# Expert rows through DRAM by indirect DMA, expert weights in loads of 512 columns, and every lower part on VectorE

## The reference

```
probs = softmax(h @ router); top_p, top_i = top_k(probs, 2); top_p /= sum(top_p)
combine = sum(one_hot(top_i) * top_p)                      # weight of a token for an expert
hid = silu(h @ w_gate[e]) * (h @ w_up[e]) * combine[..., e]   # w_gate, w_up: 8 x 1024 x 1408
f = sum over e of hid @ w_down[e]                          # w_down: 8 x 1408 x 1024
x = x + gate2 * rmsnorm(f, norms[3])
```

## Time and profile before

| | us |
|---|---|
| median of 3 timed runs | 2277.51 (2275.06 to 2282.47) |
| the profiled execution | 2269.22 |
| its span, first to last instruction | 2267.3 |
| TensorE busy | 2089.9 (92%) |
| VectorE busy | 1180.6 (52%) |
| ScalarE busy | 893.9 (39%) |
| GpSimd busy | 387.4 (17%) |
| expert loop, first product to last copy | 1619.66 to 2232.42 |
| moved by DMA | 354.66 MB |

### The profile page before, as it was taken

The page is one execution under the profiler, slowest core; times in us unless marked ns, Lnnn a source line. Parts: engine busy times, 40 slices in busy tenths (PEclk is TensorE's granted clock), DMA queues, the critical chain, the costliest instruction groups (busy, mean ns, idle before and its releaser), DMA issues.

```text
span 2267.3 us, 36209 instructions
## 1 busy us (share of the span) xinstructions
PE 2089.9 (92%) x15258; PEld 1771.2 (78%) x15258; DVE 1180.6 (52%) x1505; ACT 893.9 (39%) x1210; POOL 387.4 (17%) x274
## 2 busy tenths in 40 slices
PE   4899899999979999869989999997799999999996
PEld 2898788885549999859878888655588888888875
DVE  1955345543064342387534554214666666676774
ACT  2345522231142222233462223202466666566653
POOL 2600123220000000063003333000022222221112
PEclk7899899999979999989989999997799999999998
DMA  9322012236443434652111212645199888889981
GB/s 326 138 75 79 1 39 95 76 109 217 148 149 120 140 100 127 200 193 89 66 38 39 64 69 93 232 175 163 45 283 296 279 276 276 277 275 289 284 273 45
DMA packets 305234, 354.66 MB, mean 156 GB/s; under 512 B 4937, under 2 KB 245601, under 8 KB 304608
## 3 DMA queue, kind: packets, MB, share of 16 engines
q1 hardware_dynamic: 303456, 346.56, 46.9%
q0 software_dynamic: 1664, 6.41, 0.9%
HBM read 346.66 MB, written 6.29 MB: 156 GB/s over the span
## 4 chain that ended last, share of the span: by engine, by line
PE 79%; DVE 10%; ACT 4%; DMA 4%; issue 3%; DVEq 0%; POOL 0%; SPq 0%; ACTq 0%; POOLq 0%
PE bank L1341 6%; PE bank L1342 6%; PE bank L1343 6%; PE bank L1224 5%; PE bank L871 5%; PE bank L1096 4%; PE bank L873 4%; PE bank L872 4%; PE bank L1237 4%; PE bank L1253 4%; PE bank L1251 4%; PE bank L1252 4%; PE bank L1318 3%; PE bank L907 3%; PE bank L908 3%
## 5 line engine op out<-in xcount | busy, mean ns | idle before, releaser
L873 PE MATMUL bank<-hT_hi,ring_split 128*128 128x384 f32 x576 | 195.3, 339 | 0.0
L1402 ACT ACTIVATE ring_split<-ring 128x1024 fp32r<-128x1024 f32 (+2 forms) x86 | 119.7, 1411 | 166.9 <-DMA ring<-in_ffn_w_up 109.8
L559 POOL TENSOR_TENSOR ring_split<-ring,w_upper_a 128x1536 fp32r<-128x1536 f32 (+1 forms) x20 | 63.5, 3197 | 593.6 <-ACT w_upper_a L554 593.6
L554 ACT ACTIVATE w_upper_b<-ring 128x2048 fp32r<-128x2048 f32 (+2 forms) x80 | 124.0, 1563 | 96.5 <-PE bank L1343 96.5
L559 DVE TENSOR_TENSOR ring_split<-ring,w_upper_a 128x2048 fp32r<-128x2048 f32 (+2 forms) x60 | 135.0, 2291 | 46.4 <-ACT w_upper_a L554 46.4
L554 ACT ACTIVATE w_upper_a<-ring 128x2048 fp32r<-128x2048 f32 (+1 forms) x80 | 129.4, 1642 | 71.0 <-PE bank L1343 71.0
L2096 DVE TENSOR_TENSOR ring_split<-ring,ring_split 128x2048 fp32r<-128x2048 f32 (+1 forms) x30 | 74.1, 2503 | 145.7 <-ACT ring_split L1402 145.7
L1342 PE MATMUL bank<-ring_split,xg_hi 128*128 128x512 f32 (+1 forms) x400 | 148.6, 371 | 0.0
L871 PE MATMUL bank<-hT_hi,ring_split 128*128 128x384 f32 x384 | 141.2, 368 | 4.3 <-DVE modv L1801 2.9
L909 PE MATMUL bank<-ring_split,hT_hi 128*128 128x256 f32 x480 | 138.6, 289 | 0.0
L1402 ACT ACTIVATE work<-bank 128x256 f32<-128x256 f32 (+2 forms) x131 | 52.9, 448 | 214.9 <-PE bank L1096 86.5
(11 more groups left out here) (356 smaller groups left out, 5503.7 us busy)
## 6 DMA issues: line engine op xcount, KB each, us to landing
ring<-in_w_in SPq DMA_DIRECT2D x28, 2048.0 KB, 9.0
ring<-in_ada_w SPq DMA_DIRECT2D x24, 2048.0 KB, 10.2
ring<-in_moe_w_down SPq DMA_DIRECT2D x30, 1408.0 KB, 6.1
ring<-in_moe_w_gate SPq DMA_DIRECT2D x40, 1024.0 KB, 7.2
ring<-in_moe_w_up SPq DMA_DIRECT2D x40, 1024.0 KB, 9.7
oT<-in_moe_w_down SPq DMA_DIRECT2D x10, 1408.0 KB, 6.2
ring<-in_w_branch SPq DMA_DIRECT2D x8, 1536.0 KB, 17.5
ring<-in_ffn_w_gate SPq DMA_DIRECT2D x11, 1024.0 KB, 5.5
```

Of the source, the lines that this page charges most:

```text
L554: nc.scalar.activation(m_half(w_upper[j % 2], j, h), m_half(m_place(j), j, h), ACT.Copy).then_inc(mw_hi, 1)
L559: op.tensor_tensor(m_half(m_place(j, True), j, h), m_half(m_place(j), j, h), m_half(w_upper[j % 2], j, h).bitcast(F32), ALU.subtract).then ...
L873: last = mm(out, lo, hT_hi[:, k], start=False, stop=k == KT - 1)
```

## The change

The rows of an item and its result now pass through two DRAM tensors, `xslots` and `yslots`, of 14 x 128 rows of 1024. Both are filled with zeros once, by SP from the cleared DeltaNet state, ahead of the load of w_in block 9: xslots in layer 0, yslots in layer 1. GpSimd writes every token's row to its two slots with six indirect DMAs, SP reads the 128 rows of the next item into `xs`, and TensorE transposes them (`turn_rows`). Only item 0 is still gathered by products. SP stores each item's result to `yslots` (`store_out`). At the end GpSimd reads the two result rows of every token back with six indirect DMAs, and ScalarE and VectorE weigh and add them, and make norm, gate and residual in the row layout; the residual stays in the banks, transposed by TensorE. Selection, weighted selection, scatter and the adds of every item are gone.

Loads 0 to 5 now come in pairs: 512 columns of gate and up (the last pair 384) by 4 row tiles; loads 6 to 9 hold 512 columns of down by 6 or 5 row tiles. Gate and up go to a bank each. SiLU, gate product and the transposes of hidden are made once for each pair. VectorE makes all lower parts. What SP, GpSimd and the two row layouts do at the end is in the diff:

```diff
-            return (2, KT, 256 if j < M_GU - 1 else P) if j < M_GU else (1, FE, 256)
+            return (2, 4, 512 if j < M_GU - 2 else 384) if j < M_GU else (1, 6 - j % 2, 512)
...
+                if kind == "w" and at[1] == 9:
+                    sp.wait_ge(s_zero, at[0] + 1)
+                    sp.dma_start((xslots, yslots)[at[0]].rearrange("(i p) n -> p i n", p=P),
+                                 RX[:, 6144:7168].unsqueeze(1).to_broadcast([P, NI, D])).then_inc(zero_out, 16)
...
+                if j == M_SLOT + 1:
+                    for done in moved:
+                        sp.wait_ge(done, 32)
+                    sp.dma_start(xs, xslots[P:2 * P, :]).then_inc(xs_in, 16)
...
                     moe_load(e, j)
+                    if j == M_SLOT:
+                        store_out(i - 1)
+                        sp.wait_ge(ga_mm, 2 * i + 2)
+                        sp.dma_start(xs, slot_rows(xslots, i + 1)).then_inc(xs_in, 16)
+            store_out(last_item)
...
-            with pool.Fori(0, n_items) as i:
-                for j in POOL_U:
-                    for h in range(M_HALF):
-                        m_lower(pool, nc.gpsimd, j, h, i, mp_lo)
+            pool.wait_ge(route_ok, 5)
+            for t in range(NT):
+                for j in range(TOP_K):
+                    pool.indirect_dma_start(xslots, row_at(t, j), h2tok[:, t], None).then_inc(moved[t], 16)
...
+            pool.wait_ge(ys_out, 32 * n_items + 1)
+            link(nc.gpsimd.tensor_tensor(place2, place2, place2, ALU.subtract))
+            for t in range(NT):
+                for j in range(TOP_K):
+                    pool.indirect_dma_start(yrow[j][:, t], None, yslots, row_at(t, j)).then_inc(moved[t], 16)
...
-                            if j == 0:
-                                scatter(i)
-                            else:
-                                turn_hidden(j - 1, i)
...
-                        gather(0)
-                        turn_hidden(M_GU - 1, i)
-                        gather(1)
+                            if j in (2, 4):
+                                turn_hidden(b - 1, i)
+
+                        pe.wait_ge(xs_in, 16 * i + 16)
+                        for half in range(2):
+                            turn_rows(half)
+                        turn_hidden(M_BLK - 1, i)
...
+            def scaled(t):
+                act.wait_ge(moved[t], 64)
+                go(yrow[0][:, t], yrow[0][:, t], ACT.Copy, scale=m8[:, 8 * t:8 * t + 1]).then_inc(y_a, 1)
...
+                    v.tensor_tensor(esel, slot1.unsqueeze(1).to_broadcast([P, NT, SLOTS]), bc(rank[:, :, 0], SLOTS),
+                                    ALU.is_equal).then_inc(route_ok, 1)
...
+                        for b in range(M_BLK - 1):
+                            lower(2 * b + 2, i)
+                            if b:
+                                hidden_lower(b - 1, i)
+                            half_lower(2 * b + 3, 0, i)
+                            hidden_gate(b, i)
+                            half_lower(2 * b + 3, 1, i)
...
+            def y_add(t):
+                wait(dve, "root", DEPTH - 1, 4 + t)
+                link(v.reciprocal(vss[:, t:t + 1], vss[:, t:t + 1]))
+                link(v.scalar_tensor_tensor(yrow[0][:, t], yrow[0][:, t], vss[:, t:t + 1], grow[:, 0 if t == 0 else 1], ALU.mult, ALU.mult))
+                dve.wait_ge(xo_mm, 4 + t + 1)
+                v.tensor_tensor(yrow[0][:, t], yrow[0][:, t], banks[:, 512 * X_BANK[t]:512 * X_BANK[t] + D], ALU.add).then_inc(xo_ev, 1)
```

More of the change, by code:

```diff
@@ L1320, in gather, with turn_rows @@
                         last.then_inc(ga_mm, 1)
[L1322 to L1329 removed]
+                    def turn_rows(half):
+                        for m in range(4 * half, 4 * half + 4):
+                            last = tr(B[4 + half][:, (m % 4) * P:(m % 4 + 1) * P], xs[:, m * P:(m + 1) * P])
+                        last.then_inc(ga_mm, 1)
@@ L1382, in _ @@
                             for h in range(M_HALF):
                                 m_split(pe, j, h, i)
-                                product(out, j, h, ehid_hi, ehid_lo).then_inc(dn_mm, 1)
-                    scatter(n_items)
-                    sum_squares(layer, 4, sqP)
+                                product([B[OUT_BANK[(j - M_GU) // 2]][:, :]], j, h, ehid_hi, ehid_lo, FE).then_inc(dn_mm, 1)
                 ada_units(at["n4"], 6, ada_buf)
-            wait(pe, "xk", DEPTH, 0)
-            for t in range(NT):
-                for half in range(2):
-                    for k in range(4):
-                        last = tr(B[2 + 2 * t + half][:, k * P:(k + 1) * P], xT[:, 4 * half + k, t * P:(t + 1) * P])
-                    last.then_inc(xo_mm, 1)
+            pe.wait_ge(mod_ok, 4 * DEPTH)
@@ new lines, in _ @@
+            for q, b in enumerate((0, 1, 6, 7)):
+                g, half = divmod(q, 2)
+                for k in range(4):
+                    last = mm(B[b][:, k * P:(k + 1) * P], mod[:, DEPTH - 1, 5, 4 * half + k, g:g + 1].to_broadcast([P, P]), ident,
+                              start=True, stop=True)
+                last.then_inc(xo_mm, 1)
+            for t in range(NT):
+                if t:
+                    pe.wait_ge(y_a, 2 * t)
+                else:
+                    pe.wait_ge(ga_lo, 2 * n_items + 2)
+                for k in range(KT):
+                    last = tr(banks[:, 512 * X_BANK[t] + k * P:512 * X_BANK[t] + (k + 1) * P], xT[:, k, t * P:(t + 1) * P])
+                last.then_inc(xo_mm, 1)
@@ new lines, in item_upper @@
+                        gate_silu(M_BLK - 1, i)
+                        ahead(M_GU - 1, 0, i)
+                        hidden_upper(M_BLK - 1, i)
+                        ahead(M_GU - 1, 1, i)
+                        gathered(i + 1)
+                        for j in range(M_GU, M_GU + 2):
+                            for h in range(M_HALF):
+                                ahead(j, h, i)
+                        act.wait_ge(ys_out, 32 * i + 1)
+                        out_half(0, i)
+                        if not last:
+                            for h in range(M_HALF):
+                                ahead(M_GU + 2, h, i)
@@ L1749, in _ @@
+                        out_half(1, i)
+                        if not last:
+                            for h in range(M_HALF):
+                                ahead(M_GU + 3, h, i)
                     for j in range(2):
@@ L1757, in _ @@
                     item_upper(last_item, True)
-                    act.wait_ge(sc_ad, KT * n_items + KT + 1)
-                    for k in range(KT):
-                        square(yT, sqP, k)
+                    break
                 root(layer, 4)
@@ new lines, in place_rows @@
+                    def place_rows():
+                        link(v.tensor_scalar(nit, e_lo, float(SLOTS), -1.0, ALU.mult, ALU.add))
+                        link(v.tensor_tensor(ranked, rank, nit.unsqueeze(1).to_broadcast([P, NT, NE]), ALU.add))
+                        for pk in picks:
+                            last = v.tensor_tensor(pk, pk, ranked, ALU.mult)
+                        link(last)
+                        for j, pk in enumerate(picks):
+                            last = v.tensor_reduce(place2[:, :, j], pk, AX.X, ALU.add)
+                        link(last)
+                        v.tensor_copy(row_of, place2.rearrange("p t j -> p (t j)")).then_inc(route_ok, 1)
```

314 lines of the change are left out of this document (158 added, 156 removed).

## The result

| | before | after |
|---|---|---|
| median of the timed runs, us | 2276.99 (2275.06 to 2282.47, 4 runs) | 2141.18 (2139.86 to 2144.84, 4 runs) |
| ratio, 95% interval | | 0.9402 (0.9382 to 0.9423) |
| span of the profiled execution | 2267.3 | 2138.4 |
| expert loop, first product to end of the last copy | 613.4 | 495.2 |
| one turn of it | 61.42 | 49.53 |

The changed kernel is 6.0% faster, 135.8 us by the medians. The prediction was 2145 within 2128 to 2188.

A forecast was written before the change was run, and what follows sets the result against it. TensorE was taken to bound the expert loop, transfers next. From 2269.2 us, minus 114 (loop), 7.3 (ahead of it) and 11.2 (end), came 2136.7; with 8.3 added for the median, 2145, range 2128 to 2188.

The forecast's parts named there:

- Gather, -5.3: Expert loop, TensorE: the gather's products are on the path in full; removing them saves 5.3 us a turn.
- The waits: Expert loop, TensorE: a new 0.6 us wait before turning the last hidden tiles; the gap at the turn's end stays.
- VectorE 42.0, ScalarE 37: Expert loop: busy time a turn, VectorE 42.0 of 50 us with GpSimd's lower parts taken over, ScalarE about 37.
- Transfers: Expert loop: 18.35 MB a turn needs 47.4 us at 387 GB/s, 50.3 at 365; hidden at 387, barely.
- Ahead of the loop, -7.3: From rank to first expert product: gather starts right behind the rank; 7.3 us saved, bounds 5 and 9.
- Indirect stores: GpSimd's six row stores at the loop's start: 7 to 22 us, hidden if they end by 1636.
- The fill, 0 to 10: SP's 7.34 MB of zeros once in each layer: costs nothing, or 0 to 10 us if stores ran at half rate.
- The end, -11.2: After the last result's copy: six indirect reads, then weighing, norm and store; 11.2 us saved, bounds 15.9 and 0.5.
- (a): Expert loop: transfers bound the turn, 52.7 us at 348 GB/s, +27 us, 2172 in all; chance 0.17.
- (b): Expert loop: VectorE's order bounds, a turn of 54 us, +40 us, 2185 in all; chance 0.12.
- (c): Expert loop: 281 GB/s is a ceiling, a turn of 65.3 us, +153 us, 2298 in all, slower; chance 0.04.
- (d): Loop start and end: indirect stores hold SP's queue well past 1636, indirect reads take their upper bound; 2176, chance 0.05.

## Why the prediction was right, point by point

- **What bounds.** TensorE's order, with the transfers next: shown by both. One wait of 0.95 us removed shortened the turn by 1.23; the transfers bind at 348 GB/s (rows of 1 KB) and do not at 371 (rows of 2 KB).
- **Scatter, -7.1 a turn.** Measured 6.96 by leaving it out of the kernel before.
- **Gather, -5.3.** The sum was right and its reason incomplete. Leaving it out gives 0.1 us. The step took scatter and gather as "on the path in full", with a new wait of 0.6 in place of the gather. It did not ask what the gather covered in the kernel before, and it did not say that the first down product stands free of the last hidden block only since the down loads are cut by rows. Without that the turn is 53.3, not 49.5. The last line of the prediction named the danger in general, and the trace of before could have priced it: there the chain of five steps (SiLU, gate product, transpose, upper and lower part) ends only 1.7 us ahead of the first down product, so no more than that could be gained by leaving the gather out.
- **The waits.** The new one, +0.6, is 0.30 us idle ahead of the last hidden transposes. The gap at the turn's end was to stay at 0.52 and grew to 0.95; its cause was as stated, since aligning the halves removed it. Product counts and lengths held. The sum was 49.8, taken as 50.0; measured 49.53.
- **VectorE 42.0, ScalarE 37.** 42.05 and 38.68. The 3.12 us piece is gone, 1.755 stands in its place. By the Trainium skill, "SBUF — State Buffer", section "SBUF: two separate sides", the piece had been shut out by GpSimd's operation; the trace agrees, since the piece takes 1.755 us with GpSimd idle and 3.115 beside it in the kernel without the scatter. In the kernel before it starts at 2035.85 and ends at 2038.97, 1.6 us behind the end of GpSimd's last piece at 2037.36. But taking GpSimd's share away is worth only 0.4 to 0.6 us a turn in the changed kernel.
- **Transfers.** 47.4 us at 387 was near (the demand is 371, 384 was reached). The 365 GB/s taken for 1 KB rows was too high: rows of 1 KB give 348, which the third line of the earlier trace rows had said. Nothing hung on it, because the rows are 2 KB now. The Trainium skill, "DMA: Bandwidth & Descriptors", section "Where 436 GB/s comes from", puts a core's DRAM limit at about 358 GB/s. In this program, which runs on one core, 374 held over the eight turns from 1665.04 to 2061.50, and 384 over two turns in the kernel with one more read, so the measurement decides against it here.
- **Ahead of the loop, -7.3.** Measured 6.0. The selection (0.56 us) and TensorE's answer to it delay the gather to 0.92 us behind the rank where 0.12 was taken, and the gather took 8.2 us, not 7.8.
- **Indirect stores.** Hidden, but not with the room that was forecast. GpSimd is done with the six (0.95 to 3.00 us each and 0.30 apart) at 1630.7, but the last one lands at 1639.36, 3.4 us behind the 1636 that the prediction allowed. SP's queue waited for it, load 7 went out at 1639.82 instead of 1629 and landed at 1646.65. ScalarE took it up at 1647.52, so 0.9 us was left; load 6, which travelled beside the stores, landed 0.5 us before it was taken up at 1640.41. TensorE waited for neither: the first turn is 49.52 us.
- **The fill, 0 to 10.** 0 to about 1 in layer 1. In layer 0 the stores land at 291.4, 14 us before the load behind them goes out.
- **The end, -11.2.** Measured 6.6, the largest miss of a term. The six reads took 7.3 us as against 8.1. But they land 5.3 us behind the last issue, not 2.6, and what follows takes 12.3 us, not 9.3: VectorE works from 2124.76 to 2135.4 without a pause on steps of all three tiles, not for the last one alone.
- **The sum.** 114 + 7.3 + 11.2 = 132.5 forecast, 118.2 + 6.0 + 6.6 = 130.8 measured. Of that, 1.9 us went to a later rank, so the profiled execution is 2140.2 against the 2136.7 of the sum, 3.5 more. The 8.3 us that were then added to come to the median were no property of the kernel: in the changed kernel the median is 1 us above the profile. That error is 7.3 us the other way. So 2145 lies 3.8 us above the measured 2141.2 with two errors working against each other, which is luck. The 114 us of the loop are not, though the gather, their second largest term, came for a reason that was not given.
- **Rivals.** (a) is what the kernel is with 1 KB rows: right price, 52.7, and it does not hold with 2 KB. (b) and (c) fall by 0.95 us of waits for lower parts and 371 GB/s. (d): the stores did hold SP's queue past 1636, to 1639.4, but TensorE waited for nothing of it; its half about the reads came in part.

## What to carry to other kernels

Before counting a removed piece as saved, list which chains over the other engines run beneath it: the gather was 5.3 us of TensorE's own work and worth 0.1, because a chain of 4.4 us needed most of that cover and the lower clock behind the exposed waits took the rest, and its time was gained only by cutting a contraction so that the first part needs none of the last results. When a turn gets shorter, price again what was far from the bound: rows of 1 KB cost 3.1 us a turn at 50 us, where a turn of 61 asked for 281 GB/s of their 348.

## What the runs showed of the hardware

- Loads with rows of 1 KB (some of 768 bytes) moved 348 GB/s with the DMA share at 1.10, while ScalarE waited for them. With rows of 2 KB (some of 1.5 KB) 384 GB/s were moved over 100 us at a share of 1.06; of the 19.4 MB a turn one MB is the item's rows in and out and one the added read with rows of 1 KB.
- Behind three places TensorE ran at the lower of its two levels (1.2 in place of 2.4 GHz): after waits of 1.38 and 1.51 us close together, after one of 2.57, and after one of 2.10. Products of 256 columns were 0.21 us apart in place of 0.12 for some 3.4 us, those of 512 columns 0.43 in place of 0.23 for some 3.5. So the two waits of 2.9 us together cost 4.6. The wait of 0.95 us at each turn's start had no such tail (granted clock 1.00 over the turn).
- An indirect DMA of 128 rows of 4 KB takes GpSimd 0.95 us (stores up to 3.00) and 0.30 us to the next; the reads land 4.4 to 6.3 us after their issue, the stores 4.6 to 9.9 (median 9.1).
- A store of 7168 KB of zeros lands in 20.8 to 21.0 us.
